# Forward scores of a chunked recurrence: 32, 64, 96 or 128 keys as weights in place of 128

## The chip, the cores and the metric

The kernel runs on one core of a Trainium2 chip. A core has TensorE (PE, whose weight loads are shown apart as PEld), VectorE (DVE), ScalarE (ACT), GpSimd (POOL) and SyncE (SP, which issues most transfers). The metric is the device time of one execution in microseconds (us); lower is better. Before the change it is 2331.76 us, the median of three runs (2330.78 to 2332.65).

## What is computed

One layer of a diffusion backbone on 2048 tokens of width 1024: modulated norm, a wide input projection, a convolution half and a bidirectional gated recurrence (HGRN2) half, an output projection, then an expert-choice mixture of 16 experts and a final norm. The change is in the recurrence. For each head and direction the reference does, chunk by chunk:

```
b = cumsum(log f)                                  # decay along the tokens, per channel
scores[t, s] = sum_k q[t,k] * k[s,k] * exp(b[t,k] - b[s,k])      for s <= t, else 0
o = (q * exp(b)) @ state + scores @ v
state = exp(b_last) * state + (k * exp(b_last - b)).T @ v
```

The forward direction goes up the tokens, so a query sees the keys at or before it; the backward one is the same on the reversed tokens, so a query sees the keys at or after it.

## The kernel before, in words

The stages follow each other: modulation, convolution, heads (the recurrence), output projection, top-k, experts. `heads_stage` takes four heads of 128 channels. Per head it goes through ten units: two of 256 context tokens (forward, backward), which have no scores, and eight of 512 tokens, forward and backward in turn. All tiles hold channels on the partitions and tokens along the free side. Units of even number are forward and have buffer half `p == 0`.

In a unit of 512 tokens (four tiles of 128) the scores are built from blocks of `CH` = 32 queries. Decays are taken relative to the middle of the block, so every query block needs its own scaled copy of the keys: `KX[:, p, n * 128 : (n + 1) * 128]` holds for query block n (0 to 15 in a unit, `n % 4` in its tile) the 128 keys of its tile, scaled towards that block. GpSimd and the rest fill in only the key blocks that the query block can see and the others stay zero. `score` (L1484 to L1498 of the listing below) is one matmul: weights are that slice of KX (128 channels by 128 keys), moving operand the 32 queries of the block in `E`, and the result, 128 keys by 32 queries, goes into columns n * 32 of the PSUM tile `pat` (shown as `pout` in the profile, of which it is a part). Both operands are f32, and an f32 matmul is carried out as two pairs of weight load and matmul.

What is read of `pat`: `mask` (DVE, L1339) copies it into `AT` through a triangular mask, so only the entries of visible keys are copied; AT was set to zero once, at the start of the stage.

The order is written out by hand. PE's stream in `one(h, ...)` is, for i = 0 to 9: state updates of unit i, outputs of unit i-1, transposes of unit i+1, scores of unit i+1; between nearly all of these stand one by one the 24 bf16 matmuls of `project` (L1473, 128x512, or 128x256 for context units) for unit i+3. So while the 16 scores run, each stands between two bf16 matmuls of the projection. In the last head there is nothing left to project for the last units. Scores of a unit wait for three things: queries scaled on DVE (`qh_ok`, L1313), keys scaled on GpSimd (`kx_ok`, L1076) and the mask of the unit before (`at_ok`).

Of the kernel before, what the change touches and what calls it, by code (L numbers as in the profile page):

```python
# [27 lines left out]
P = 128  # L28
# [14 lines left out]
CH = 32  # L43
# [27 lines left out]
def wait(engine, sem, value):  # L71


    if not (isinstance(value, int) and value <= 0):
        engine.wait_ge(sem, value)
# [741 lines left out]
def heads_stage(nc, K, I, scr, GW_):  # L817
# [7 lines left out]
    BLK = P // CH  # L825
# [8 lines left out]
    def at(h, i):  # L834
        return h + i // NU, i % NU
# [21 lines left out]
    def X(h, i):  # L857
        h, i = at(h, i)
        return h * NX + max(0, i - 2)
# [22 lines left out]
    with nc.cleanup_on_exit(), ExitStack() as ctx:  # L882
# [15 lines left out]
        KX = m.sb("KX", [P, 2, ST * BLK * P])  # L898
# [15 lines left out]
        pu, pk, pat = pout[0][:, 0], pout[0][:, 1], pout[1][:, 1]  # L914
# [63 lines left out]
        with nc.Block() as block:  # L978
# [484 lines left out]
            def _(pe):  # L1463
# [22 lines left out]
                def score(h, i, n):  # L1486
                    h, i = at(h, i)
                    p = i % 2
                    if UNITS[i][1] < 0:
                        return  # L1490
                    if n == 0:
                        wait(pe, qh_ok, X(h, i) + 1)
                        wait(pe, kx_ok, X(h, i) * 3 + 3)
                        wait(pe, at_ok, X(h, i))
                    ins = nc.tensor.matmul(pat[:, n * CH:(n + 1) * CH], KX[:, p, n * P:(n + 1) * P],  # L1495
                                           E[:, p, n * CH:(n + 1) * CH], start=True, stop=True)
                    if n == ST * BLK - 1:
                        ins.then_inc(at_ps, 1)  # L1498
# [49 lines left out]
                def one(h, prev, cur, nxt):  # L1548
                    for i in range(NU):
                        ahead = there(i + 3, prev, cur, nxt)  # L1550
                        for mm in range(ST):
                            if cur:
                                update(h, i, mm)
                            if ahead:
                                project(h, i + 3, mm)
                        for mm in range(2 * ST):
                            if there(i - 1, prev, cur, nxt):
                                output(h, i - 1, mm)
                            if ahead and mm < ST:
                                project(h, i + 3, ST + mm)  # L1560
                            if mm == ST - 1:
                                for r, j in due(h, i, 9, prev, cur):
                                    mean(r, j)
                        near = there(i + 1, prev, cur, nxt)
                        if near:
                            transposes(h, i + 1)
                        for n in range(ST * BLK):
                            if ahead:
                                project(h, i + 3, 2 * ST + n)
                            if near:  # L1570
                                score(h, i + 1, n)
# [1106 lines left out]
```

## Time and profile before

| | |
|---|---|
| median of three runs | 2331.76 us |
| the profiled execution | 2329.09 us, span on the core 2327.0 us |
| TensorE busy over the span | 2194.1 us (94%) |
| VectorE busy | 1607.7 us (69%) |
| ScalarE busy | 1041.9 us (45%) |
| GpSimd busy | 486.8 us (21%) |
| score matmuls (L1495) | 1024, from 583.5 to 977.7 us of the span |
| their weight loads | 1024, 166.1 us busy, 198 ns mean |
| mean granted TensorE clock | 0.973 of full speed |

Start times in the trace are from the start of the span. A matmul's record ends when its result is out, so matmuls that follow each other overlap in the records; what one costs in a dense stream is the distance from its start to the next start. A form such as "128*128 128x32" gives the rows and columns of the array that hold weights (channels * keys) and then the moving operand. A weight load (PEld) may run while the matmul before it still streams.

### The profile page before, as it was taken

What the parts mean: (1) busy time and instruction counts of PE and PEld (TensorE: products, weight loads), DVE (VectorE), ACT (ScalarE), POOL (GpSimd) and SP (SyncE); (2) the same over time, 40 slices, a digit from 0 to 9 for tenths busy, and PEclk for the clock granted to TensorE, in tenths of its full rate; (3) what the DMA queues carried; (4) which work ended last, traced back from release to release, by engine and by line L of the source; (5) the groups of instructions that cost most, each with busy time, mean ns of one, the idle gap of its engine ahead of it and who ended that gap; (6) DMA issues with size and microseconds to landing.
All of it is one profiled execution on the core that took longest, in us unless ns stands there. A gap on an engine that the chain in (4) does not pass through costs nothing. (4 is left out here: it accounts for less than half of the span.)

```text
span 2327.0 us, 38579 instructions
## 1 busy us (share of the span) xinstructions
PE 2194.1 (94%) x14740; PEld 1486.6 (64%) x14885; DVE 1607.7 (69%) x2235; ACT 1041.9 (45%) x1329; POOL 486.8 (21%) x535
## 2 busy tenths in 40 slices
PE   6799999999999898999986999999999999999995
PEld 3344444444878796845543777777777777777773
DVE  2839999784678787865556666666666666666666
ACT  3611002355566666644532444434444444443444
POOL 0610001012556565400003111011110111101111
PEclk9899999999999999999987999999999999999998
DMA  9341002454021120374544676676766776667776
GB/s 343 80 85 37 19 19 86 127 159 148 6 55 49 46 56 24 116 250 149 167 155 176 222 240 218 223 233 224 227 227 214 238 231 232 220 218 233 235 230 267
DMA packets 216932, 377.16 MB, mean 162 GB/s; under 512 B 38147, under 2 KB 79619, under 8 KB 216333
## 3 DMA queue, kind: packets, MB, share of 16 engines
q1 hardware_dynamic: 198702, 317.38, 40.7%
q0 software_dynamic: 16528, 56.47, 9.0%
q10 hardware_dynamic: 1616, 2.16, 0.3%
q8 instruction: 54, 0.88, 0.2%
q14 instruction: 32, 0.26, 0.0%
HBM read 313.44 MB, written 62.54 MB: 162 GB/s over the span
## 5 line engine op out<-in xcount | busy, mean ns | idle before, releaser
L91 PE MATMUL pgu<-xhi,mwlo 128*128 128x256 bf16 x2048 | 558.2, 273 | 0.0
L90 PE MATMUL pgu<-xlo,mwhi 128*128 128x256 bf16 x2048 | 558.2, 273 | 0.0
L89 PE MATMUL pgu<-xhi,mwhi 128*128 128x256 bf16 x2048 | 558.2, 273 | 0.0
L2414 DVE TENSOR_TENSOR mwlo<-mwst,mwhi 128x2048 bf16<-128x2048 f32 x187 | 426.7, 2282 | 0.0
L2311 ACT ACTIVATE mwhi<-mwst 128x2048 bf16<-128x2048 f32 x186 | 350.8, 1902 | 0.1
L2319 ACT ACTIVATE thb<-pgu 128x256 f32<-128x256 f32 x128 | 49.1, 384 | 546.7 <-PE pgu L91 546.7
L655 DVE SCALAR_TENSOR_TENSOR co<-u,taps,co 128x1984 f32<-128x1984 f32 (+22 forms) x120 | 234.1, 1951 | 3.7
L2425 DVE SCALAR_TENSOR_TENSOR thb<-thb,pgu 128x256 f32<-128x256 f32 x128 | 53.7, 420 | 258.1 <-ACT thb L2319 258.1
L90 PEld LDWEIGHTS pgu<-xlo,mwhi 128*128 128x128 bf16 x2048 | 200.4, 98 | 24.5
L89 PEld LDWEIGHTS pgu<-xhi,mwhi 128*128 128x128 bf16 x2048 | 200.3, 98 | 24.4
L91 PEld LDWEIGHTS pgu<-xhi,mwlo 128*128 128x128 bf16 x2048 | 200.4, 98 | 23.2
L2247 POOL TENSOR_TENSOR mpflag<-mpflag 1x1 f32<-1x1 f32 x46 | 37.5, 815 | 845.4 <-DVE ysb L2441 579.4
L2584 PE MATMUL pd<-mwhi,flo 128*128 128x512 bf16 x511 | 193.7, 379 | 0.8
L2583 PE MATMUL pd<-mwlo,fhi 128*128 128x512 bf16 x497 | 188.4, 379 | 2.9 <-DVE flo L2433 1.4
L1495 PEld LDWEIGHTS pout<-E,KX 128*128 128x128 f32 x1024 | 166.1, 198 | 33.9 <-issue 13.6
L2582 PE MATMUL pd<-mwhi,fhi 128*128 128x512 bf16 x481 | 182.3, 379 | 4.2 <-DVE ysb L2441 4.1
L1495 PE MATMUL pout<-E,KX 128*128 128x32 f32 x1024 | 154.7, 243 | 19.4 <-DVE E L1313 11.1
L2441 DVE SCALAR_TENSOR_TENSOR ysb<-pd,gate,g 128x512 f32<-128x512 f32 x64 | 47.9, 748 | 84.5 <-PE pd L2584 84.5
L1473 PE MATMUL pj<-hhi,wst 128*128 128x512 bf16 (+1 forms) x306 | 103.0, 361 | 1.6 <-PEq L406 1.6
L1473 PE MATMUL pout<-hhi,wst 128*128 128x512 bf16 (+1 forms) x287 | 100.9, 373 | 0.2
L1285 DVE TENSOR_TENSOR_SCAN B<-segm,E 128x512 f32<-128x512 f32 (+1 forms) x40 | 58.2, 1454 | 56.1 <-ACT E L1132 56.1
L89 PE MATMUL pout<-hhi,whi 128*128 128x512 bf16 x251 | 95.1, 379 | 0.3
(376 smaller groups left out, 4302.5 us busy)
## 6 DMA issues: line engine op xcount, KB each, us to landing
mwst<-in_w_gate SPq DMA_DIRECT2D x32, 2048.0 KB, 8.9
mwst<-in_w_up SPq DMA_DIRECT2D x32, 2048.0 KB, 7.9
mwst<-in_w_down SPq DMA_DIRECT2D x32, 2048.0 KB, 10.6
wst<-in_w_in SPq DMA_DIRECT2D x28, 512.0 KB, 6.0
big<-in_ada_w SPq DMA_DIRECT2D x5, 2048.0 KB, 13.7
s_rows<-row SPq DMA_DIRECT2D x16, 520.0 KB, 5.7
u<-in_ada_w SPq DMA_DIRECT2D x8, 1024.0 KB, 6.7
xt<-in_x SPq DMA_DIRECT2D x16, 512.0 KB, 4.4
```

Source lines behind the costliest of these rows:

```text
L89: nc.tensor.matmul(out, lh, rh, start=(first and k == 0), stop=False)
L90: nc.tensor.matmul(out, lh, rl, start=False, stop=False)
L91: ins = nc.tensor.matmul(out, ll, rh, start=False, stop=(last and k == n - 1))
L655: nc.vector.scalar_tensor_tensor(o, i, taps[:, c, k:k + 1], o, ALU.mult, ALU.add).then_inc(tap_ok, 1)
L1285: nc.vector.tensor_tensor_scan(B[:, p, way], segm[:, 0:n], E[:, p, way], 0.0, ALU.mult, ALU.add)\
L1473: ins = nc.tensor.matmul(pj[i % 2][:, 0:n], w, x, start=(mm == 0), stop=(mm == 3 * KD - 1))
L1495: ins = nc.tensor.matmul(pat[:, n * CH:(n + 1) * CH], KX[:, p, n * P:(n + 1) * P], E[:, p, n * CH:(n + 1) * CH], start=True, stop=True)
L2311: nc.scalar.activation(whi[:, b, ks], wst[:, b % NS, ks], ACT.Copy).then_inc(w_hi, 1)
L2414: nc.vector.tensor_tensor(wlo[:, b, ks], wst[:, b % NS, ks], whi[:, b, ks], ALU.subtract)\
L2582: nc.tensor.matmul(pd[q % 2][:], fh, whi[:, 4 + c, k, :], start=(k == 0), stop=False)
L2583: nc.tensor.matmul(pd[q % 2][:], fh, wlo[:, 4 + c, k, :], start=False, stop=False)
L2584: last = nc.tensor.matmul(pd[q % 2][:], fl, whi[:, 4 + c, k, :], start=False, stop=(k == KD - 1))
```

## The change

For the forward direction (`p == 0`) the weights of query block n are only the first `keys` = 32, 64, 96 or 128 keys of its slice of KX, and the result goes only to that many partitions of `pat`. The backward direction keeps 128. The number of matmuls and loads, their order and all semaphores stay as they are; no work on another engine changes.

```diff
@@ -1492,7 +1492,8 @@
                         wait(pe, qh_ok, X(h, i) + 1)
                         wait(pe, kx_ok, X(h, i) * 3 + 3)
                         wait(pe, at_ok, X(h, i))
-                    ins = nc.tensor.matmul(pat[:, n * CH:(n + 1) * CH], KX[:, p, n * P:(n + 1) * P],
+                    keys = (n % BLK + 1) * CH if p == 0 else P
+                    ins = nc.tensor.matmul(pat[0:keys, n * CH:(n + 1) * CH], KX[:, p, n * P:n * P + keys],
                                            E[:, p, n * CH:(n + 1) * CH], start=True, stop=True)
                     if n == ST * BLK - 1:
                         ins.then_inc(at_ps, 1)
```

On PE, in the scores of the first forward unit of a head, the built program has this (a row is an instruction with its result's shape; `pout<-E,KX` is a score, `pout<-hhi,wst` a projection):

```order
L1473 MATMUL pout<-hhi,wst 128x512
L1496 MATMUL pout<-E,KX 32x32
L1473 MATMUL pout<-hhi,wst 128x512
L1496 MATMUL pout<-E,KX 64x32
L1473 MATMUL pout<-hlo,wst 128x512
L1496 MATMUL pout<-E,KX 96x32
L1473 MATMUL pout<-hhi,wst 128x512
L1496 MATMUL pout<-E,KX 128x32
```

Before, the same rows stood there with 128x32 in each score; nothing moved. The built program also gives each matmul the part of the array that it is laid on, in steps of 32, 64 or 128 rows and columns: the scores with 32 keys are laid on 128x32, those with 64 on 128x64, those with 96 and 128 and all matmuls around them on 128x128. Before, all scores were on 128x128. There are 4 heads x 4 forward units x 16 = 256 forward scores, 64 of each width.

## Rows read from the trace of the kernel before

**Rows 1.** The page, part 1: busy time and share of each engine.
```profile
PE 2194.1 (94%) x14740; PEld 1486.6 (64%) x14885; DVE 1607.7 (69%) x2235; ACT 1041.9 (45%) x1329; POOL 486.8 (21%) x535
```

**Rows 2.** Line L1495, two units after each other (ns min/median/max, first and last start).
```profile
L1495 PE MATMUL pout<-E,KX x32: 192/234/276, 604.7 to 610.0; 128*128 128x32 f32 x32
...
L1495 PE MATMUL pout<-E,KX x32: 192/234/276, 615.3 to 620.7; 128*128 128x32 f32 x32
```

**Rows 3.** Timeline of PE, full clock (start us, us, operation, idle before it).
```profile
589.15 0.30 PE L1495 MATMUL pout<-E,KX 128*128 128x32 f32 x2
589.29 0.38 PE L1473 MATMUL pout<-hhi,wst 128*128 128x512 bf16 x1
589.51 0.30 PE L1495 MATMUL pout<-E,KX 128*128 128x32 f32 x2
```

**Rows 4.** Timeline of PE's weight loads at the same place.
```profile
589.29 0.41 PEld L1495 LDWEIGHTS pout<-E,KX 128*128 128x128 f32 x2
589.54 0.18 PEld L1473 LDWEIGHTS pout<-hhi,wst 128*128 128x128 bf16 x1
```

**Rows 5.** Line L805, f32 with 128 weight columns (ns min/median/max).
```profile
L805 PE MATMUL pb<-sq,mean_cw x8: 592/592/697, 443.7 to 527.2; 128*128 128x512 f32 x8
```

**Rows 6.** Timeline of PE in the convolution stage: one-column weights after full ones.
```profile
524.50 0.38 PE L91 MATMUL pout<-hhi,wlo 128*128 128x512 bf16 x1
524.80 1.02 PE L762 MATMUL pout<-msum,ones 128*1 128x512 f32 x2
```

**Rows 7.** Timeline of the loads there.
```profile
524.80 0.09 PEld L762 LDWEIGHTS pout<-msum,ones 128*1 128x1 f32 x2 [0.42 <-issue]
```

**Rows 8.** Timeline of PE in the convolution stage: full weights after one-column ones.
```profile
549.42 1.01 PE L763 MATMUL pout<-adab,ident 4*1 4x512 f32 x2
550.37 0.39 PE L89 MATMUL pout<-hhi,whi 128*128 128x512 bf16 x1
```

**Rows 9.** Timeline of the loads there.
```profile
550.37 0.10 PEld L89 LDWEIGHTS pout<-hhi,whi 128*128 128x128 bf16 x1 [0.86 <-issue]
550.38 0.10 PEld L90 LDWEIGHTS pout<-hlo,whi 128*128 128x128 bf16 x1
```

**Rows 10.** Timeline of PE, last head: scores without projections between.
```profile
964.27 1.98 PE L1495 MATMUL pout<-E,KX 128*128 128x32 f32 x17
```

**Rows 11.** Stretches with busy time of PE, PEld, DVE, ACT, POOL; then granted clock, DMA.
```profile
585.00:588.40 3.40, 3.40 (x16) 3.02 (x15) 0.95 (x2) 0.48 (x2) 3.02 (x3) 0.50 0.00 0
...
707.90:714.70 6.80, 5.89 (x26) 5.21 (x27) 6.63 (x15) 2.48 (x5) 2.54 (x3) 0.50 0.20 40
...
817.10:820.50 3.40, 3.40 (x17) 2.95 (x16) 3.29 (x10) 2.03 (x4) 1.38 (x2) 0.50 0.02 5
...
967.30:974.10 6.80, 6.80 (x33) 6.80 (x33) 5.85 (x13) 0.62 (x2) 4.85 (x5) 0.50 1.02 407
```

**Rows 12.** Timeline of PE at half clock.
```profile
586.38 0.47 PE L1495 MATMUL pout<-E,KX 128*128 128x32 f32 x2
...
587.08 0.47 PE L1495 MATMUL pout<-E,KX 128*128 128x32 f32 x2
```

**Rows 13.** Timeline of PE: waits in the second head.
```profile
691.51 1.12 PE L1541 MATMUL hpm<-sqb,mean_p 128*128 128x512 f32 x2 [1.39 <-ACT sqb L1164]
...
708.81 0.39 PE L1495 MATMUL pout<-E,KX 128*128 128x32 f32 x1 [3.72 <-DVE E L1313]
...
762.22 0.41 PE L1495 MATMUL pout<-E,KX 128*128 128x32 f32 x2 [0.71 <-POOL KX L1076]
```

**Rows 14.** Line L1495, first and last forward unit of the second head.
```profile
L1495 PE MATMUL pout<-E,KX x32: 192/276/297, 681.7 to 687.2; 128*128 128x32 f32 x32
...
L1495 PE MATMUL pout<-E,KX x32: 195/236/276, 753.2 to 757.1; 128*128 128x32 f32 x32
```

**Rows 15.** Timeline of DVE: the mask after the first forward scores of the second head.
```profile
691.53 0.72 DVE L1339 COPY_PREDICATED AT<-msk,pout 128x512 f32<-128x512 uint32 x1
```

**Rows 16.** Timeline of ACT: the exponential from which the keys of 762.22 are scaled.
```profile
756.07 0.63 ACT L1143 ACTIVATE B<-B 128x512 f32<-128x512 f32 x1
```

## Prediction

> **What bounds the kernel now.** I read the page's first part, then line L1495 by units, then PE's timeline in the heads stage beside that of its weight loads, then stretches with the granted clock, and last the waits of PE. The page says that TensorE is busy 94% of the span and the next engine 69% [rows 1]. That alone decides nothing, because a matmul's record is longer than its share of the stream. What decides is the pace of the units: in the first head the scores of one unit begin at 604.7 and those of the next at 615.3, 10.6 us later, and no idle time stands ahead of any of the 32 score matmuls in either [rows 2]. There PE sets the pace, and what a score costs on PE is paid in full. The edited instructions are the scores of the forward units: 256 of 512 calls, each two loads and two matmuls.
>
> **What a score costs now.** At full clock the pattern is bf16 matmul, score pair, bf16 matmul. The bf16 one starts at 589.29 and the pair at 589.51, 0.216 us for 512 columns; one pattern to the next is 589.15 to 589.51, 0.357 us before rounding [rows 3]. So a pair costs 0.142. Two matmuls of 32 columns don't need that. The loads explain it: the first load starts with the bf16 matmul and is hidden under it; the second can start only when the first score matmul has taken its weights, and the second matmul waits for it; the next bf16 load starts at 589.54 and is hidden again [rows 4]. Thus one f32 load of 128 columns is exposed per score. How long it is: line L805, 128 columns and f32, has records of 592 ns with the load hidden and 697 where it isn't, so 0.105 to 0.107 us [rows 5]. With one column nothing is to be seen: two such matmuls take 1.02 us, which is 0.43 for the first stream and 0.59 for the second record [rows 6]. I take the load as proportional to columns: 0.027, 0.053, 0.080 and 0.107 us for 32, 64, 96 and 128. Two score matmuls start at least 0.028 apart (their own streams: 0.43 us x 32/512 = 0.027).
>
> The Trainium skill, "TensorE: Matmul & The Clock Gate", section on LDWEIGHTS, has the load's time as its columns over 1.2 GHz, 107 ns for 128 and 27 for 32. The trace agrees at both ends. By that rule alone the change is a gain; it is the first rival below.
>
> **What the change adds.** The 32-key scores are laid on 128x32 of the array and the 64-key ones on 128x64, between bf16 matmuls on 128x128. The trace has such a change of layout in the convolution stage. A 512-column bf16 matmul starts at 524.50, its stream ends 0.213 later; the load for one-column weights, which otherwise would have started with it, starts at 524.80, and the load row has 0.42 us of idle time ahead of it with no releaser named [rows 6, 7]. That is 0.308 unrounded, so 0.095 after the end of the stream, and the load isn't hidden. The way back costs as much: two one-column matmuls start at 549.42, their streams end at 550.28, and the full bf16 load starts at 550.37 [rows 8, 9]; the bf16 matmul behind it streams some 0.015 later, when the next load starts (550.38). So each change of layout stops PE for 0.093 to 0.095 us and bares the load behind it. It isn't f32 against bf16 that does it: the scores of now alternate with bf16 without a stop [rows 3, 4].
>
> The Trainium skill, "TensorEngine Tiling (Array Packing)", Key Properties, says that changing the tiling mode drains TensorE, and names no price. The rows above are its price here. The same page's speedup for few weight columns needs different tiles working side by side, and here all scores sit on the first.
>
> **The sum per tile of 128 queries, full clock.**
> - 32 keys: bf16 matmul and stop 0.308, load 0.027, first matmul to second 0.028, second 0.027, stop 0.093, restart 0.015: 0.498 against 0.357, so +0.141. The second load (0.027) fits under the first matmul.
> - 64 keys: loads 0.053 each, the second partly bare: 0.308 + 0.053 + 0.055 + 0.027 + 0.093 + 0.015 = 0.551, so +0.194.
> - 96 keys: laid on 128x128 as before, no stop, second load 0.080 in place of 0.107: -0.027.
> - 128 keys: 0.
> Together +0.308 us per tile, +1.23 per unit of four tiles. There are 16 forward units. The last one, in the last head, has no projections between: 17 matmuls took 1.98 us there [rows 10], about 0.112 each, 0.89 per tile. After the change a tile is 0.093+0.027+0.028+0.027 and 0.093+0.053+0.055+0.027 and 0.093+0.080+0.080+0.027 and 0.214, also 0.90: no change. The other 15 give 18.5.
>
> Part of this runs at half clock (0.50 of full speed, which is 1.2 GHz [rows 11]): 3.4, 6.8 and 3.4 us in the first, second and third head fall on its first or second forward unit, of the 6.8 the first 0.9 before the scores; for the last head I assume 3.4 again. There a pattern takes 0.70 us [rows 12], twice as much. Loads and streams double; the stop I put at 0.13 (by its share of a record, an estimate between 0.095 and 0.19). That makes +0.44 per tile in about 6 of the tiles, 0.8 us more. In all 19.3 us on PE.
>
> **What is hidden.** PE doesn't set the pace everywhere. In the second to fourth head other engines do from the head's first forward scores to the next forward ones: PE waits 1.39 us at 691.51 for ScalarE and 3.72 at 708.81 for DVE [rows 13]. The mask that needs the scores which ended at 687.2 ran on DVE only at 691.53 [rows 14, 15], so they may end 1.2 us later without DVE noticing. I take the 1.23 of that unit as hidden in three heads: -3.7. And before the last backward scores of a head PE waits 0.71 us at 762.22 for keys from GpSimd, whose chain goes back to an exponential at 756.07, which began before the forward scores ahead of it were through (753.2 to 757.1) [rows 13, 14, 16] and needs nothing of them. There a delay of 1.23 costs only about 0.5; three heads have it: -2.1. The 3.72 at 708.81 lies ahead of the second forward unit and covers nothing of its cost. Nothing else changes: DVE, ScalarE and GpSimd have the same work, no transfer is moved, and PE is only later, so masks (queued ahead of the next unit's DVE work) come later with it. The net is 19.3 - 3.7 - 2.1 = **+13.5 us**.
>
> The profiled execution would go from a span of 2327.0 to 2340.5 and from 2329.09 to 2342.6 us; the median of the runs shown lies 2.7 us above it, so it would be 2331.76 + 13.5 = **2345 us**.
>
> **Bounds.** With no cover the sum is 19.3 (2351). If the narrow loads took the full 0.107, the 32- and 64-key scores would cost 0.16 and 0.11 more and the 96-key ones 0.03: +0.30 per tile, 18 us in all at most (2363 with the present cover). If they took nothing, the three would cost 0.03, 0.08 and 0.05 less: -0.16 per tile, 10 us in all (2335). The one-column rows and the 128-column rows lie on a line, so I stay with proportion. Layout 128x64 is in no row; I take 128x32's price, as the nearest.
>
> **Rivals.**
> - *The loads get shorter and nothing stops* (a stop only where one-column or one-row weights are involved). Then a tile saves 0.080 + 0.053 + 0.027 = 0.160, 60 tiles 9.6 us; at the units where PE waits anyway the wait only grows (three heads, two units each, 6 x 0.64 = 3.8 not gained), leaving about 6: 2326. For it: no row shows 32 or 64 columns. Against it: [rows 6 to 9] show the stop with nothing else changed. With four changes of layout per tile the net per tile is -0.068 us plus four stops, so a stop under 0.017 us decides for it.
> - *Only 128x32 stops.* The 64-key score then gains 0.053: +0.141 - 0.053 - 0.027 = +0.06 per tile, 3.7 us, 1 of it hidden: 2334.
> - *The slower PE is absorbed*, because another engine would set the pace soon after. For it: the waits of [rows 13]. Against it: [rows 2], and that the others get more time per unit, not less. 2334 or less.
> - *The clock falls.* The stops thin out the matmul stream; at 707.9, in its wait of 3.72 us, PE's clock fell to 0.50 for 6.8 us, and it fell at 967.3 in the scores without projections [rows 10, 11, 13]. If it fell once in each of the 12 units that now run at 1.0, for 3.4 us each, some 1.7 us are lost in each: +20 more, 2365. Against it: here the projections go on between the scores, which they don't do at either of those two places.
>
> **How the numbers follow.** The forecast has 0.76, the clock 0.07, only 128x32 stopping 0.03, absorption 0.05, the gain 0.09. The likeliest case with its own unknowns goes from 2338 to 2355 (cover 6 us more or none, loads a fourth off). A range that holds the time 8 times in 10 can leave out the gain and most of the clock case: 2337 to 2356. A measurement here tells about 0.2% (4.7 us) from no change, so faster means under 2327.1, slower over 2336.4. Faster: 0.08. Within: 128x32 alone, absorption and the weaker part of the gain, 0.09. Slower: the forecast and the clock, 0.83.
>
> **What would show it.** In the changed profile the loads of forms 128*32 and 128*64 should each start 0.09 us after the stream before them ended, with idle time ahead of them; their patterns should take 0.50 and 0.55 us, that of 96 keys 0.33. The 16 forward scores of a unit at full clock should go from 5.4 to 6.6 us from first to last start, and the pace of two units (forward and backward) from 21.2 to 22.4; backward units should stay. The waits of 1.39 and 0.71 us should be all but gone, that of 3.72 should stay. Experts and all later stages should have the same lengths. I am wrong if the 64-key loads start with the matmul before them, if forward units keep 10.6 us, or if the clock's row shows 0.50 where it now has 1.0.

## The result and the profile after

The change made the kernel slower. The median of four runs is 2356.35 us (2353.12 to 2359.02) against 2331.27 us for the kernel before (four runs, 2329.0 to 2332.65); the ratio is 1.0108, with a 95% interval of 1.009 to 1.0125. The forecast was 2345, so +13.5 us where +25 was measured, and the time lies just past the top of the range (2356). The direction was right, and so was the mechanism at full clock; the term for half clock was much too small.

The page after, part 1, answers to [rows 1]: PE has the same number of instructions and 25 us more busy time.
```profile
PE 2219.0 (94%) x14740; PEld 1480.9 (63%) x14885; DVE 1595.7 (68%) x2235; ACT 1041.1 (44%) x1329; POOL 486.8 (21%) x535
```

At full clock the pattern is as forecast. This is PE's timeline after, in the first head, over one tile (start us, us, operation):
```profile
612.97 0.38 PE L1473 MATMUL pout<-hhi,wst 128*128 128x512 bf16 x1
613.28 0.25 PE L1496 MATMUL pout<-E,KX 128*32 128x32 f32 x2
613.46 0.39 PE L1473 MATMUL pout<-hlo,wst 128*128 128x512 bf16 x1
613.78 0.30 PE L1496 MATMUL pout<-E,KX 128*64 128x32 f32 x2
614.01 0.39 PE L1473 MATMUL pout<-hhi,wst 128*128 128x512 bf16 x1
614.24 0.28 PE L1496 MATMUL pout<-E,KX 128*96 128x32 f32 x2
614.35 0.38 PE L1473 MATMUL pout<-hhi,wst 128*128 128x512 bf16 x1
```
And the loads at the same place (the bracket is idle time of the load row):
```profile
613.28 0.14 PEld L1496 LDWEIGHTS pout<-E,KX 128*32 128x32 f32 x2 [0.24 <-issue]
...
613.78 0.19 PEld L1496 LDWEIGHTS pout<-E,KX 128*64 128x64 f32 x2 [0.23 <-issue]
...
614.01 0.39 PEld L1496 LDWEIGHTS pout<-E,KX 128*96 128x96 f32 x2
```
Against [rows 3, 4]: where the layout changes, the load no longer starts with the bf16 matmul but 0.31 us after it, behind idle time, for 32 and for 64 keys alike; the 96-key load starts with its bf16 matmul at 614.01 as before. From bf16 start to bf16 start it is 0.49 us with 32 keys, 0.55 with 64, 0.34 with 96 (forecast 0.50, 0.55, 0.33).

By units, line L1496 in a backward unit and the forward one behind it (ns min/median/max, first and last start), which answers to [rows 2]:
```profile
L1496 PE MATMUL pout<-E,KX x32: 192/234/276, 600.8 to 606.2; 128*128 128x32 f32 x32
...
L1496 PE MATMUL pout<-E,KX x32: 192/220/276, 611.5 to 618.1; 128*32 128x32 f32 x8, 128*64 128x32 f32 x8, 128*96 128x32 f32 x8, 128*128 128x32 f32 x8
```
Last score to last score is 11.9 us where it was 10.6, and the backward unit keeps its 10.6.

The waits of PE in the second head, answering to [rows 13]:
```profile
700.83 1.13 PE L1542 MATMUL hpm<-sqb,mean_p 128*128 128x512 f32 x2 [0.33 <-ACT sqb L1164]
...
718.12 0.28 PE L1496 MATMUL pout<-E,KX 128*32 128x32 f32 x2 [3.71 <-DVE E L1313]
...
777.16 0.31 PE L1496 MATMUL pout<-E,KX 128*128 128x32 f32 x2
```
1.39 us became 0.33, 3.72 stayed 3.71, and the 0.71 us before the last backward scores are gone.

The clock is where the profile differs from the forecast. Stretches after, with busy time of PE, PEld, DVE, ACT and POOL, then the granted clock, which answer to [rows 11]:
```profile
588.30:598.40 10.10, 9.77 (x40) 6.54 (x40) 2.09 (x4) 2.12 (x3) 5.35 (x7) 0.50 0.00 0
...
718.00:731.50 13.50, 12.90 (x53) 8.52 (x55) 9.18 (x18) 5.09 (x9) 6.10 (x8) 0.50 0.10 22
731.70:735.00 3.30, 3.30 (x26) 3.07 (x26) 2.62 (x4) 0.58 (x1) 3.08 (x2) 1.00 0.00 0
830.60:844.20 13.60, 13.13 (x54) 8.67 (x55) 9.08 (x18) 5.46 (x9) 6.47 (x8) 0.50 0.09 19
943.30:956.80 13.50, 13.03 (x54) 8.96 (x55) 8.92 (x19) 5.99 (x9) 6.99 (x8) 0.50 0.09 19
...
746.00:753.50 7.50, 7.36 (x53) 4.91 (x53) 4.37 (x15) 3.68 (x6) 4.28 (x6) 1.00 0.73 225
```
Before, these half-clock stretches (1.2 GHz) lasted 3.4, 6.8, 3.4 and 3.4 us. After, they last 10.2 and three times 13.6, and the clock is back only when the unit's scores are over (they end at 729.4, the clock rises at 731.6). This was the last of the prediction's signs of being wrong: 0.50 where the same scores had 1.0. The narrow scores at 746 to 753 run at full clock: once up, it stays. The stretch of before in the fourth head, which the rows ahead of the prediction don't have, and the second forward unit of the second head, before and after:
```profile
922.90:926.30 3.40, 3.40 (x18) 2.95 (x17) 3.26 (x11) 1.96 (x4) 1.19 (x1) 0.50 0.11 22
...
L1495 PE MATMUL pout<-E,KX x32: 192/276/402, 708.8 to 717.1; 128*128 128x32 f32 x32
...
L1496 PE MATMUL pout<-E,KX x32: 230/279/402, 718.1 to 729.4; 128*32 128x32 f32 x8, 128*64 128x32 f32 x8, 128*96 128x32 f32 x8, 128*128 128x32 f32 x8
```
Its 16 scores take 11.3 us where they took 8.3. These are single profiles; the other runs agree with them: the mean granted clock is 0.965 to 0.969 in the four runs after and 0.972 to 0.979 in all runs of the kernel before that stand beside the experiments.

Where the 25 us are, from last score to last score of each unit in the two profiles (head by head, each difference with that of the backward unit behind it):

| units | measured | forecast |
|---|---|---|
| five forward units at full clock, 512-column projections | 5 x 1.25 = 6.25 | 6.2 |
| first forward unit of heads 2 to 4 (waits take it up) | 0.0 | 0 |
| fourth forward unit of heads 1 to 3 | 0.5 | 1.6 |
| second forward unit of heads 2 to 4 (half clock) | 4.0 + 4.9 + 5.0 = 13.85, summed before rounding | 4.3 |
| first forward unit of head 1 (half clock) | 3.85 | 1.4 |
| last head's last scores | 0.7 | 0 |
| sum | 25.2 | 13.5 |

The profiled execution took 2359.02 us (span 2357.0), 2.7 more than the median. Its first score is 2.9 us later than before, ahead of everything that was changed: it has a half-clock stretch in the convolution stage (137.7 to 141.1 us) that the profile of before lacks. The profile of the 65-key kernel below has one at the same place (137.2 to 140.6 us) and nothing of the change lies ahead of it, so I take it as a difference between executions.

### The profile page after: what moved, and what is told of

The parts are those of the page before. It is cut to its first block and busy times, and to the rows that moved or that the text cites. A ratio compares the mean times of both kernels' runs of the same rounds, so it can differ in the third digit from the quotient of the medians.

```text
span 2357.0 us, 38579 instructions
## 1 busy us (share of the span) xinstructions
PE 2219.0 (94%) x14740; PEld 1480.9 (63%) x14885; DVE 1595.7 (68%) x2235; ACT 1041.1 (44%) x1329; POOL 486.8 (21%) x535
## 5 line engine op out<-in xcount | busy, mean ns | idle before, releaser
L1496 PEld LDWEIGHTS pout<-E,KX 128*128 128x128 f32 (+3 forms) x1024 | 152.6, 183 | 61.6 <-issue 40.8
L1496 PE MATMUL pout<-E,KX 128*128 128x32 f32 (+3 forms) x1024 | 155.2, 242 | 20.9 <-DVE E L1313 10.8
L1473 PE MATMUL pout<-hhi,wst 128*128 128x512 bf16 (+1 forms) x287 | 106.0, 389 | 0.2
L90 PE MATMUL pout<-hlo,whi 128*128 128x512 bf16 x251 | 95.1, 379 | 0.3
```

The lines of the kernel that those rows point to most:

```text
L90: nc.tensor.matmul(out, lh, rl, start=False, stop=False)
L1473: ins = nc.tensor.matmul(pj[i % 2][:, 0:n], w, x, start=(mm == 0), stop=(mm == 3 * KD - 1))
L1496: ins = nc.tensor.matmul(pat[0:keys, n * CH:(n + 1) * CH], KX[:, p, n * P:n * P + keys], E[:, p, n * CH:(n + 1) * CH], start=True, stop=True)
```

## The experiments

Theory A: PE pays for each change between layouts (128x128 to 128x32 or 128x64 and back), not for narrow weights, and where the clock is already at half, the stops delay its return. Theory B: short loads or few result partitions are slow in themselves. Theory C: the excess is spread over the stage. All ratios are against runs of the kernel before that stand beside the experiment's, on the same chip. The edits are against the changed kernel; where several one-line edits share a block, each + line is a run of its own. A stop is one change of layout, so a narrow score between two projections has two.

**65 keys in place of 32 and 64.**
```diff
-                    keys = (n % BLK + 1) * CH if p == 0 else P
+                    keys = max(65, (n % BLK + 1) * CH) if p == 0 else P
```


> Forward scores with 65, 65, 96 and 128 keys in place of 32, 64, 96 and 128, so that all stay on the 128x128 layout while the loads stay short. The output is still the reference's. Theory A (the price is the change of layout, the width alone saves): no stops; per tile 0.053+0.053+0.027 = 0.13 us less than before wherever PE sets the pace, some 36 to 40 tiles, plus the last unit: about 6 us under the kernel before, 2325; the half-clock stretches are as long as before (6.8 us at the second forward unit of the second head). Theory B (short loads or narrow results are themselves slow on PE): slower than before by 5 us or more, with patterns over 0.357 us. The 65-key pattern should take 0.30 us under A.

Measured: 2324.76 us against 2329.71, ratio 0.9981 (0.9972 to 0.999). PE's timeline in the first head:
```profile
606.08 0.25 PE L1496 MATMUL pout<-E,KX 128*65 128x32 f32 x2
606.17 0.38 PE L1473 MATMUL pout<-hlo,wst 128*128 128x512 bf16 x1
606.38 0.25 PE L1496 MATMUL pout<-E,KX 128*65 128x32 f32 x2
606.47 0.38 PE L1473 MATMUL pout<-hhi,wst 128*128 128x512 bf16 x1
606.69 0.28 PE L1496 MATMUL pout<-E,KX 128*96 128x32 f32 x2
```
The 65-key pattern takes 0.30 us, as Theory A had it; no stop. Its half-clock stretches:
```profile
707.30:714.00 6.70, 6.11 (x30) 4.66 (x31) 6.53 (x15) 2.17 (x5) 2.63 (x3) 0.50 0.19 40
813.10:819.80 6.70, 5.80 (x29) 4.39 (x30) 6.53 (x15) 2.47 (x5) 2.44 (x3) 0.50 0.19 39
918.90:925.60 6.70, 5.86 (x30) 4.41 (x31) 6.53 (x15) 2.71 (x5) 2.52 (x3) 0.50 0.21 43
```
6.8 us in heads 2 to 4, not 13.6, and none in the first head. Theory B falls. In heads 3 and 4 it was 3.4 us before, so a stretch can be 3.4 us longer in one profile than in another without any stop. This version is faster than both kernels, by 5 us (6 was expected) and by some 30.

**The change in some units only.**
```diff
-                    keys = (n % BLK + 1) * CH if p == 0 else P
+                    keys = (n % BLK + 1) * CH if p == 0 and i >= 6 else P     # third and fourth forward units
+                    keys = (n % BLK + 1) * CH if p == 0 and i < 6 else P      # the other run: first and second
```


> The change only in the third and fourth forward unit of each head (units 6 and 8), which run at full clock before and after. Theory A (stops cost 0.29 us per tile at full clock; what came on top of the forecast is half clock that lasts longer in the units where the clock had fallen anyway): +1.16 us in each of four third units, +0.2 in three fourth ones, and up to 2 in the last head's: +5 to +8 us, 2337 to 2339. Theory C (the excess is spread over all units, or comes from elsewhere in the stage): about half of the whole change's 25 us, +12.

Measured: 2334.67 us, ratio 1.0022 (1.0012 to 1.0031), so +5.

> The change only in the first and second forward unit of each head (units 2 and 4), the complement of the run before. Theory A: +3.9 and +1.2 in the first head, nothing in the first unit of the other heads, +4.0, +5.0 and +5.1 in their second units: about +19 us, 2350, with half-clock stretches of 10 to 14 us there instead of 3.4 to 6.8. Theory C: about +12. If the long half-clock stretches were chance, +7.

Measured: 2346.68 us, ratio 1.0076 (1.0062 to 1.0091), so +17, 2 less than expected. The two add up to 22 of the 25 us, and they are far from equal: half of the forward units carry three quarters of the 22. Theory C falls. In the second run the half-clock stretches of heads 2 to 4 are again 10 to 14 us; in the first, which has no stops there, they are 3.4, 6.8 and 6.8 us.

**One width at a time.**
```diff
-                    keys = (n % BLK + 1) * CH if p == 0 else P
+                    keys = CH if p == 0 and n % BLK == 0 else P               # 32 alone
+                    keys = 2 * CH if p == 0 and n % BLK == 1 else P           # 64 alone
+                    keys = 2 * CH + 1 if p == 0 and n % BLK == 1 else P       # 65 alone
```


> Only the first query block of each tile gets narrow weights (32 keys, layout 128x32); the others take all 128 keys. Half the changes of layout. Theory A by the stops alone: +0.141 us per tile, 8.5 us on PE, about 3 of it hidden: +6, 2337. If the half-clock stretches lengthen as in the whole change, +12 or more on top of the same stops: 2348. Theory B: like A, no distinction.

Measured: 2339.23 us, ratio 1.0042 (1.0025 to 1.006), +9.5, between the two figures. At full clock a forward unit takes 11.19 us from last score to last score (10.61 before), +0.145 per tile. The half-clock stretches are 13.6, 10.2 and 10.2 us in heads 2 to 4, but still 3.4 in the first head, where one narrow score with its two stops (at 585.6 us) lies inside the stretch.

> Only the second query block of each tile gets narrow weights (64 keys, layout 128x64); the others take all 128. Theory A (a change of layout to 128x64 stops PE as one to 128x32 does): +0.19 us per tile at full clock, so 16 scores from 5.38 to 6.16 us from first to last start; with longer half-clock stretches as in the 32-key run, +10 to +13 us in all. Theory D (only 128x32 stops): -0.053 us per tile, 5.17 us, and faster by 2.

Measured: 2344.87 us, ratio 1.0059 (1.0042 to 1.0076), +15. The first forward unit at full clock:
```profile
L1496 PE MATMUL pout<-E,KX x32: 192/233/276, 606.8 to 613.0; 128*128 128x32 f32 x24, 128*64 128x32 f32 x8
```
6.2 us from first to last score, as Theory A had it; a change to 128x64 stops PE like one to 128x32. Theory D falls. The total is 2 us over the expected 10 to 13; the half-clock stretches are 6.8 us in the first head and 10.2, 13.6 and 13.6 in the others.

> The same as the run before with 65 keys in place of 64, so one column more and the layout 128x128. The output is still the reference's. Theory A: -0.053 us per tile, 16 scores in 5.17 us, half-clock stretches as before, about 2 us faster. Theory B (a short load or a result on fewer partitions is what costs): as slow as with 64.

Measured: 2324.61 us, ratio 0.9977 (0.9968 to 0.9987), 5 us faster. The same unit:
```profile
L1496 PE MATMUL pout<-E,KX x32: 192/208/276, 604.1 to 609.3; 128*128 128x32 f32 x24, 128*65 128x32 f32 x8
```
5.2 us. One weight column more, one layout less, and the kernel is 20 us faster than with 64. The gain of 5 us is more than the 2 us that the loads account for; in its profile the last head has 3.4 us of half clock where the profile of before has 6.8 and 3.4, which may be chance: in the four runs that leave the last head's fourth forward unit as it was (first and second units only, and the three with single tiles below), that unit and the backward one behind it take between 1.5 us less and 0.7 us more than before.

**Where in a half-clock unit the stops stand.**
```diff
-                    keys = (n % BLK + 1) * CH if p == 0 else P
+                    keys = (n % BLK + 1) * CH if p == 0 and i == 4 and n < BLK else P                  # first tile
+                    keys = (n % BLK + 1) * CH if p == 0 and i == 4 and n >= (ST - 1) * BLK else P      # last tile
+                    keys = (n % BLK + 1) * CH if p == 0 and i == 4 and BLK <= n < 3 * BLK else P       # second and third
```


> The change only in the first of the four tiles of each head's second forward unit (unit 4), which in the second to fourth head runs at half clock: four changes of layout per unit, at the start of its scores. Theory A1 (stops during half clock delay its end): 0.4 us per unit for the stops, and the half-clock stretches last 10 us in place of 3.4 to 6.8 in some or all of the three heads: +4 to +9 us. Theory A2 (the clock is late for another reason than these stops, such as the many that follow, or chance): +1.5 us.

Measured: 2330.49 us, ratio 1.0001 (0.9992 to 1.0011): no difference. The stretches of the second head:
```profile
708.70:715.40 6.70, 5.25 (x24) 4.12 (x25) 6.53 (x15) 3.02 (x5) 2.44 (x3) 0.50 0.20 40
715.50:719.00 3.50, 3.50 (x30) 3.25 (x29) 2.21 (x4) 1.80 (x4) 2.96 (x4) 1.00 0.02 5
```
As long as before, and 3.4 us in the third and fourth head too. But only the second head puts the question: there all four stops lie at half clock. In the third and fourth head the scores begin at full clock, at 816.7 and 922.6 us, and the four changes of layout are over by 817.4 and 923.4, before the clock falls at 817.9 and 923.7. So against Theory A in its plain form (any stop during half clock delays its return) stands the one stretch of the second head. The total can't decide it: 3.4 us more of half clock in one head would cost some 1.7 us, which lies within the interval.

> The same four changes of layout per unit, but in the last tile of unit 4's scores, by when the clock is back at full in the kernel before. Theory A1: stops at full clock only, 0.29 us per unit, +1 us in all, half-clock stretches of 3.4 to 6.8 us as before. Theory A2: the same +1.5 as with the first tile.

Measured: 2329.47 us, ratio 1.0 (0.999 to 1.0009): no difference. Theory A1 expected +1 and A2 +1.5, and the interval doesn't tell them apart.

> The change only in the second and third tile of each head's unit 4: eight changes of layout per unit, in the stretch in which the clock comes back before the change. Theory A3 (the clock doesn't come back while scores with stops are running, whatever came ahead of them): the half-clock stretches of the second to fourth head last 10 us or more and end only after the narrow tiles; +3 us for the stops and +1.5 to 3.5 per head for the clock, +7 to +12 us. Theory A2 (the long stretches of the whole change have another cause): stretches of 3.4 to 6.8 us, +3 us.

Measured: 2337.43 us, ratio 1.003 (1.0017 to 1.0042), +7. The stretches of its three heads:
```profile
710.50:724.00 13.50, 12.00 (x49) 9.02 (x51) 9.35 (x19) 4.96 (x9) 5.61 (x8) 0.50 0.10 21
...
823.10:833.20 10.10, 9.88 (x41) 7.07 (x42) 6.92 (x16) 4.06 (x8) 5.06 (x7) 0.50 0.04 8
932.30:942.40 10.10, 9.88 (x42) 7.07 (x42) 7.27 (x17) 4.46 (x8) 5.35 (x7) 0.50 0.05 9
```
With stops in the second and third tile, around the place where the clock returned before, it stays at half for 13.6 and 10.2 us. The cost is that of the clock more than of the eight stops: the unit takes 0.63 us more in the first head, where it runs at full clock, and 3.1 to 3.3 in the others. What matters seems to be whether stops stand where the clock would otherwise come back. Their number isn't separated from their place, though: this run has eight in a unit, the two before it have four.

The stretches at the second forward unit of heads 2 to 4, over all profiles:

| kernels | stretches, us |
|---|---|
| no stops there, or in one tile only: before, 65 keys, third and fourth units, 65 alone, first tile, last tile | 3.4 or 6.8, all 18 |
| stops in two tiles or all, scores and projections alternating: the change, first and second units, 32 alone, 64 alone, second and third tile, and the alternating run below | 10.2 or 13.6, all 18 |
| stops in all tiles, the narrow scores side by side: the last run below | 10.2, 3.4, 6.8 |

**Changes of layout against narrow scores.** Both blocks with 64 keys; in the second run the two scores stand next to each other, in forward units.
```diff
-                    keys = (n % BLK + 1) * CH if p == 0 else P
+                    keys = max(2, n % BLK + 1) * CH if p == 0 else P          # both runs
...
-                            if ahead:
+                            if ahead and (n % BLK != 1 or i % 2 == 0):        # second run
                                 project(h, i + 3, 2 * ST + n)
                             if near:
                                 score(h, i + 1, n)
+                            if ahead and n % BLK == 1 and i % 2:
+                                project(h, i + 3, 2 * ST + n)
```


> 64 keys for the first two query blocks of each tile, 96 and 128 for the others, every score between two projections as ever: four changes of layout per tile, all to and from 128x64. The output is still the reference's. Stops of about 0.095 us each and bared loads: 2 x 0.194 - 0.027 = +0.36 us per tile, 16 scores in 5.38 + 1.44 = 6.8 us at full clock; with long half-clock stretches about +28 us.

Measured: 2357.91 us, ratio 1.0118 (1.0101 to 1.0135), +27; 16 scores at full clock:
```profile
L1496 PE MATMUL pout<-E,KX x32: 192/233/277, 613.3 to 620.1; 128*64 128x32 f32 x16, 128*96 128x32 f32 x8, 128*128 128x32 f32 x8
```


> The same widths, but in forward units the second score of each tile stands directly behind the first and the projection that stood between them comes after both: two changes of layout per tile in place of four, the same loads and matmuls. If the price goes by changes of layout: bf16 and stop 0.308, four loads of 0.053 of which each is bare, last matmul 0.027, stop 0.093, restart 0.015 and the second bf16 0.216, 0.88 us against 0.714, less 0.027 for the third block: +0.14 us per tile, 16 scores in about 5.9 us at full clock, half of the time or less of what the alternating order costs. If it goes by narrow scores whatever their order: 6.8 us.

Measured: 2336.24 us, ratio 1.003 (1.0018 to 1.0041), +5.6:
```profile
L1496 PE MATMUL pout<-E,KX x32: 192/223/276, 605.7 to 611.6; 128*64 128x32 f32 x16, 128*96 128x32 f32 x8, 128*128 128x32 f32 x8
```
Its timeline shows one stop ahead of four narrow matmuls:
```profile
607.00 0.38 PE L1473 MATMUL pout<-hhi,wst 128*128 128x512 bf16 x1
607.31 0.42 PE L1496 MATMUL pout<-E,KX 128*64 128x32 f32 x4
607.66 0.39 PE L1473 MATMUL pout<-hlo,wst 128*128 128x512 bf16 x1
```
Same loads, same matmuls, half the changes: 6.8 us became 5.9, and the whole lost four fifths of its price, because the half-clock stretches are shorter too (10.2, 3.4 and 6.8 us in heads 2 to 4). At full clock the price goes by changes of layout. The part that comes by the clock doesn't go by their number alone: the runs with 32 and with 64 keys alone also have two changes in each tile, and cost 9.5 and 15 us where this one costs 5.6. Why the order of this run lets the clock come back sooner is open.

## Why the prediction was right and wrong

- **Stop at a change of layout, 0.095 us into it and 0.093 out of it:** right, in size too. The rows of the convolution stage carried over to 32 columns and to 64. The comparison of 64 and 65 keys shows that it comes with the layout, and not with the short load. The rule of the Trainium skill, "TensorEngine Tiling (Array Packing)", Key Properties, that a change of tiling mode drains TensorE agrees with these stops. So does, at full clock, the load time by columns in the Trainium skill's "TensorE: Matmul & The Clock Gate", LDWEIGHTS: a forward unit with one 65-key score in each tile took 10.40 us where it had taken 10.61, 0.053 us per tile. The stops outweighed this saving.
- **Sum per tile, 0.308 us:** measured 0.313 (1.25 us per unit over four tiles). Of it 0.145 comes from the 32-key score (forecast 0.141) and 0.197 from the 64-key one (0.194), each from the run with that width alone.
- **Cover:** close. The 1.23 us of the first forward unit in heads 2 to 4 was hidden in full, as said. In the fourth unit more was hidden than forecast (0.5 us in all against 1.6): the wait of 0.71 us went, and the backward unit behind it, which had waited for GpSimd, came to 8.1 us instead of 9.1 to 9.3. This error made the forecast too high, by 1.1 us.
- **Half clock: this is the step that failed.** "Part of this runs at half clock" took the stretches of the old trace, 3.4 and 6.8 us, as given and added 0.8 us for the stops in them. It gave no reason why they would stay as long. They grew to 10.2 and 13.6 us, and the units in which they lie cost 17.7 us where 5.7 was forecast. The missing 12 us are all there: of the other rows of the table, cover was forecast 1.1 us too high, the last head's last scores 0.7 too low, and the full clock hit. The rival *The clock falls* named the right agent and looked in the wrong place: it asked whether stops would bring the clock down in the units at full clock (they didn't in any), not whether they would keep it down where it had already fallen. Its figure, +20 us, isn't what happened either.
- **Range:** its top, 2356, came from the forecast's own unknowns plus part of the clock case. The growth of the half-clock stretches should have been among the bounds: they came out two to four times as long. That the time lies only 0.35 us past the top is luck: the range had no term for what happened.
- **Rivals:** the gain without stops is refuted by the loads after the change, the one with stops for 128x32 alone by the 64-key run. Absorption by another engine is refuted where PE sets the pace: forward units take 1.25 us more and backward units keep 10.6 us.

What stays open: by what the stops keep the clock at half, and why the stretch is 10.2 us in some heads and 13.6 in others. Stops in a stretch aren't always enough: in the first head of the run with 32 keys alone and in the third head of the run with adjacent scores it stayed at 3.4 us. The last head's 0.7 us and the 65-key runs' last microsecond are of the size by which that place varies without being changed.

## What to carry to other kernels

A matmul with few weight columns isn't free to place: if 64 columns or fewer put it on another part of the array than its neighbours, each change costs about 0.1 us and bares the load behind it, which here was more than the shorter load saved. Trim weights to 65 columns or more. Putting the narrow matmuls next to each other lowers the price, but here it still left a loss of 5.6 us. And when an edit puts stops into PE's stream, look in the profile for places where the clock is at half already: there the same edit can cost several times its price (here 4.0 to 5.0 us for a unit that cost 1.25 at full clock), because the clock comes back later.

## What the runs showed of the hardware

- The stop doesn't double at half clock. In the profile after, bf16 start to narrow load is 0.54 us, of which 0.43 is the stream, so about 0.11 (0.095 at full clock; the prediction took 0.13):
```profile
718.34 0.61 PE L1473 MATMUL pout<-hhi,wst 128*128 128x512 bf16 x1
...
718.88 0.29 PEld L1496 LDWEIGHTS pout<-E,KX 128*64 128x64 f32 x2 [0.44 <-issue]
```
- Four stops at the start of one half-clock stretch left its length unchanged (6.8 us), eight in the tiles around the clock's return went with stretches of 10.2 or 13.6 us in place of 3.4 or 6.8 (+7 us in all). I had expected the first to matter as well.
- Scores of 65 keys keep the layout of 128 and save in proportion to their columns: 0.30 us per pattern against 0.357.
